# Moving one of six weight buffers 64 bytes along the partition

## The chip, the cores and the metric

The kernel runs on one core of one Trainium2 chip. The metric is the device time of one execution in microseconds (us); lower is better.

## The reference

Two layers of a first block (convolution, block attention, gated linear attention, a feed-forward part with a short convolution) run over 256 tokens of width 1024, then two layers of a second block (adaptive modulation, two feed-forward half steps, neighbourhood and windowed attention with a context of 256 tokens). Nearly all of the arithmetic is in products of the tokens with large float32 weight matrices; cut to these:

```python
def reference(x, ..., w_in, w_out, ffn_w_up, ffn_w_down, ...):
    for l in range(2):             # first block
        p = rms_norm(x, norm_mix_g[l]) @ w_in[l]
        y = mixers(p)              # convolution, block attention, linear attention
        x = x + y @ w_out[l]
        u = causal_depthwise_conv(rms_norm(x, norm_ffn_g[l]) @ ffn_w_up[l], ...)
        x = x + (silu(u[..., :2816]) * u[..., 2816:]) @ ffn_w_down[l]
    x = rms_norm(x, final_g)
    for l in range(2):             # second block, x and ctx
        x, ctx = half_step(x, ..., w_up_2[l, 0], w_down_2[l, 0]), half_step(ctx, ...)
        px, pc = modulate(norm(x)) @ w_in_2[l], modulate(norm(ctx)) @ w_in_2[l]
        attended = attention(px, pc)
        x = x + gate * (attended @ w_out_2[l])
        x = half_step(x, ..., w_up_2[l, 1], w_down_2[l, 1])
    return x
```

## The kernel before

All weight matrices are laid out by the host as one stream of 510 units of 128 partitions x 1024 float32 (512 KB each). Every unit goes through the same four steps.

- SyncE loads it into slot `g % 6` of the ring `W_raw` (`load`, L825), once TensorE is done with unit `g - 6`.
- ScalarE copies it, rounded to fp32r, into slot `g % 4` of the ring `W_hi` (`split`, L1505), once TensorE is done with unit `g - 4`.
- VectorE writes raw minus high into `W_lo` (`split`, L1881). `W_lo` has the same addresses as `W_raw`: the subtraction is in place, slot by slot.
- TensorE multiplies. The inputs are split into a high and a low part in the same way (`H_hi`, `H_lo` and `HID` of a stream, A for the tokens and B for the context), and each product of 128 x 128 weights with 256 columns of input takes three matmuls in one accumulation group (`three`, L977 to L979): low weights with high inputs, high weights with low inputs, high with high. The weights are the stationary operand, loaded by a LDWEIGHTS each, the inputs the moving one.

A visit is the use of one unit by one stream: 8 such groups of three, 24 matmuls. There are 744 visits, since many units of the second block serve both streams, A and B, in turn. In 28 visits (`token`, L1031 to L1034) the roles are swapped: the inputs are stationary and the weights move. I call these token visits and the others feature visits. Of the 744 visits 124 use a unit in the last slot (`g % 6 == 5`). TensorE runs the visits in the fixed order of the list `ORDER`, and between them it does attention and normalisation matmuls.

The addresses within a partition are written out by hand, from an aligned base. Every slot of the weight rings begins at a multiple of 4096 bytes; the input buffers begin 192 bytes past a multiple of 1024, and so does each of their rows of 256 elements:

```python
        W_hi = at("W_hi", 0, [P, HIGH, UNIT], F32R)
        W_raw = at("W_raw", 16 * K, [P, RAW, UNIT])
        W_lo = at("W_lo", 16 * K, [P, RAW, UNIT], F32R)
        AA, AB = 72 * K + 192, 124 * K + 192
        for s, h_at, x_at, arena in ((A, 40 * K + 192, 150 * K + 256, AA), (B, 56 * K + 192, 158 * K + 256, AB)):
            s.H_hi = at("H_hi" + n, h_at, [P, KT, SEQ], F32R)
            s.H_lo = at("H_lo" + n, h_at + 8 * K, [P, KT, SEQ], F32R)
            s.HID = at("HID" + n, arena, [P, 6, 2, 512], F32R)
```

The pieces of weights that a matmul loads begin at multiples of 512 bytes within the slot. So while a LDWEIGHTS reads its piece, the matmul before it reads inputs whose address is 192 bytes further on, counted modulo 512; only where a feature visit follows a token visit, or the other way round, does one pair have another distance (both operands at a multiple of 512, or both 192 past one).

Of the kernel before, what the change touches and what calls it, by code (L numbers as in the profile page):

```python
# [6 lines left out]
F32 = mybir.dt.float32  # L7
F32R = mybir.dt.float32r
# [3 lines left out]
ACT = mybir.ActivationFunctionType  # L12
AX = mybir.AxisListType

P = 128
# [12 lines left out]
UNIT = 1024  # L28
RAW = 6
HIGH = 4  # L30
# [147 lines left out]
MIX1_OUT = [1, G, 3, G, 5, G, 7, G, G, 0, 2, 4, 6]  # L178
GLUE = 13
LATE_BIAS = 6  # L180
FIRST_KV = 17
B_FIRST = {24: 21, 25: 23}
A_FIRST = {24: 3, 25: 5}
# [130 lines left out]
def make_order():  # L314
# [20 lines left out]
    def b_may():  # L335
# [5 lines left out]
        if ia < len(a) and a[ia].stage.kind == "att2" and a[ia].i == 0 and b[ib].stage.kind == "in2" \  # L341
                and b[ib].i >= FIRST_KV and (len(b[ib].stage.steps) - b[ib].i) % 3 == 0:
            return False
# [11 lines left out]
    def a_may():  # L355
# [4 lines left out]
            and not (a[ia].stage.kind == "att2" and a[ia].i == 0 and ib < len(b) and b[ib].stage.kind == "in2"  # L360
                     and not (b[ib].i >= FIRST_KV and (len(b[ib].stage.steps) - b[ib].i) % 3 == 0))

# [240 lines left out]
def build_kernel(nc, xT, ctxT, wstream, adastream, par, const, imask, cond, outT):  # L603
    with ExitStack() as ctx:  # L604
        K = 1024
# [5 lines left out]
        def at(name, off, shape, dt=F32, limit=SPACE):  # L611
            size = int(np.prod(shape[1:])) * (2 if dt == BF16 else 4)
            assert off + size <= limit - (base - whole), (name, off, size)
            return nc.alloc_sbuf_tensor_at(name, shape, dt, offset=base + off)

        W_hi = at("W_hi", 0, [P, HIGH, UNIT], F32R)
        W_raw = at("W_raw", 16 * K, [P, RAW, UNIT])
        W_lo = at("W_lo", 16 * K, [P, RAW, UNIT], F32R)
        A_raw = at("A_raw", 166 * K + 256, [P, ADA_RING, UNIT])
        PROD = at("PROD", 174 * K + 256, [P, 2, UNIT], BF16)  # L620
        SC = at("SC", 178 * K + 256, [P, 2, D])
# [16 lines left out]
        S = Semaphores(lambda name: ctx.enter_context(nc.semaphore(name)))  # L638
# [109 lines left out]
        def wait(eng, sem, value):  # L748

            if isinstance(value, int) and value <= 0:  # L750
                return
            eng.wait_ge(sem, value)
# [58 lines left out]
        @block.sync  # L811
        def _(sp):
            half = KT // 2
            sp.dma_start(A.X[:, 0:half, :], xT[:, 0:half, :]).then_inc(S.x_in, 16)
            sp.dma_start(A.X[:, half:KT, :], xT[:, half:KT, :]).then_inc(S.x_in, 16)
            sp.dma_start(CON[:, 0:CON_HEAD], const[:, 0:CON_HEAD]).then_inc(S.head_in, 16)
            sp.dma_start(PAR[:, 0:PAR_HEAD], par[:, 0:PAR_HEAD]).then_inc(S.head_in, 16)

            def load(g):

                if g >= RAW:
                    s, n = FREED[g - RAW]
                    sp.wait_ge(streams[s].sem.done, n)
                u = UNITS[g]
                sp.dma_start(W_raw[:, g % RAW, :], wstream[u * P:u * P + P, :]).then_inc(S.raw_in[g % RAW], 16)  # L825

            def load_ada(t):

                wait(sp, S.mod_sums, t - ADA_RING + 1)
                sp.dma_start(A_raw[:, t % ADA_RING, :], adastream[P * t:P * t + P, :])\  # L830
                    .then_inc(S.ada_in[t % ADA_RING], 16)

            for g in range(AHEAD):
                load(g)
            sp.dma_start(CON[:, CON_HEAD:], const[:, CON_HEAD:]).then_inc(S.con_in, 16)
            sp.dma_start(PAR[:, PAR_HEAD:], par[:, PAR_HEAD:]).then_inc(S.par_in, 16)
            for g in range(AHEAD, RAW):
                load(g)
            sp.dma_start(MASKI[:, :], imask).then_inc(S.mask_in, 16)
            sp.dma_start(SC[:, :, :], cond).then_inc(S.cond_in, 16)  # L840
            sp.dma_start(B.X[:, :, :], ctxT).then_inc(S.ctx_in, 16)
            for t in range(ADA_RING):
                load_ada(t)
            t, due = ADA_RING, 0
            for v in ORDER:
                if v.final and v.g + RAW < TOTAL["u"]:
                    load(v.g + RAW)
                if v.final:
                    for _ in range(due):
                        if t < ADA_UNITS:  # L850
                            load_ada(t)
                            t += 1
                    due = v.ada
            st = STAGES["A"][-1]
            sp.wait_ge(A.sem.evac, st.old.tok)
            sp.dma_start(outT[:, 0:half, :], A.X[:, 0:half, :]).then_inc(S.stored, 16)
            sp.wait_ge(A.sem.upd, st.upd + 1)
            sp.dma_start(outT[:, half:half + 2, :], A.X[:, half:half + 2, :]).then_inc(S.stored, 16)
            sp.wait_ge(A.sem.evac, st.old.tok + 1)
            sp.dma_start(outT[:, half + 2:KT, :], A.X[:, half + 2:KT, :]).then_inc(S.stored, 16)  # L860
            sp.wait_ge(S.stored, 48)
# [3 lines left out]
        def _(pool):  # L865
# [5 lines left out]
            def bias_table(l):  # L871

                pool.memset(BT[:, :, :], BIG).then_inc(S.bt_low, 1)
                pool.wait_ge(S.bt_low, l + 1)
                o = _par[f"rpb{l}"]
                rows = par[0:64, o:o + 48].rearrange("(h r) e -> h r e", h=2)
                for c in range(64):
                    c0 = min(max(c - 8, 0), 48)
                    r = 15 + c0 - c
                    for h in range(2):  # L880
                        pool.dma_start(BT[64 * h + c:64 * h + c + 1, c0:c0 + 16, :], rows[h:h + 1, r:r + 16, :])\
                            .then_inc(S.bt_in, 16)
# [27 lines left out]
            def ffn(s, st):  # L910
                for i in range(len(st.steps)):
                    if i == LATE_BIAS and st.blk == 1 and st.l == DEPTH - 1:
                        pool.wait_ge(s.sem.done, st.v)
                        bias_table(0)
                    if i == LATE_BIAS and s is A and st.blk == 2 and st.l == 0 and st.ffn == 1:
                        pool.wait_ge(s.sem.done, st.v)
# [35 lines left out]
        def _(pe):  # L952
# [17 lines left out]
            def weights():  # L970
                g = now.visit.g
                pe.wait_ge(S.w_lo, g + 1)
                return W_lo[:, g % RAW, :], W_hi[:, g % HIGH, :]

            def three(out, wl, wh, xl, xh, start, stop):

# [4 lines left out]
            def plain(s, st, b, q, hw):  # L981

                wl, wh = weights()
                for t in range(2):
                    for k in range(4):
                        kt = 4 * (q % 2) + k
                        if t == 0 and q < 2:
                            pe.wait_ge(s.sem.h_ready, hw(kt))
                        c = slice(256 * k + P * t, 256 * k + P * t + P)
                        mm = three(b[:, 2 * (q // 2) + t, :], wl[:, c], wh[:, c], s.H_lo[:, kt, :], s.H_hi[:, kt, :],  # L990
                                   kt == 0 and t == 0, kt == 7)
                mm.then_inc(s.sem.done, 1)

            def early(s, st, b, q):

                wl, wh = weights()
                for t in range(2):
                    for k in range(4):
                        kt = 4 * (q % 2) + k
                        if t == 0 and q < 2:  # L1000
                            pe.wait_ge(S.h0_ready, KT * st.early + kt + 1)
                        c = slice(256 * k + P * t, 256 * k + P * t + P)
                        mm = three(b[:, 2 * (q // 2) + t, :], wl[:, c], wh[:, c], H0_lo[:, kt, :], H0_hi[:, kt, :],
                                   kt == 0 and t == 0, kt == 7)
                mm.then_inc(s.sem.done, 1)
# [490 lines left out]
        def _(act):  # L1496
            def split(g):

                if g >= TOTAL["u"]:
                    return  # L1500
                act.wait_ge(S.raw_in[g % RAW], 16 * (g // RAW + 1))
                if g >= HIGH:
                    s, n = FREED[g - HIGH]
                    act.wait_ge(streams[s].sem.done, n)
                act.activation(W_hi[:, g % HIGH, :], W_raw[:, g % RAW, :], ACT.Copy).then_inc(S.w_hi, 1)  # L1505

            def evacuated(s, tok):

# [357 lines left out]
        def _(dve):  # L1866
# [9 lines left out]
            def split(g):  # L1876

                if g >= TOTAL["u"]:
                    return
                dve.wait_ge(S.w_hi, g + 1)  # L1880
                dve.tensor_tensor(W_lo[:, g % RAW, :], W_raw[:, g % RAW, :], W_hi[:, g % HIGH, :].bitcast(F32),  # L1881
                                  ALU.subtract).then_inc(S.w_lo, 1)

            def ada():
# [683 lines left out]
            for n, v in enumerate(ORDER):  # L2568
                if 2 <= n < 2 + AHEAD:
                    split(n - 2)  # L2570
                if n == FIRST_STEPS:
                    dve.wait_ge(S.par_in, 16)
                    dve.wait_ge(S.con_in, 16)
                    for l in range(DEPTH):
                        o = _par[f"sink{l}"]
# [159 lines left out]
```

## Time and profile before

| | |
|---|---|
| median of 3 runs | 2533.37 us (2530.72 to 2538.22) |
| the profiled execution | 2531.44 us |
| its span, first to last instruction | 2529.6 us |
| TensorE matmul busy | 2391.1 us, 95% |
| TensorE weight load busy | 2318.8 us, 92% |
| VectorE busy | 1660.9 us, 66% |
| ScalarE busy | 995.8 us, 39% |
| GpSimd busy | 187.9 us, 7% |
| mean granted TensorE clock | 0.967 of full speed |
| DMA | 352.78 MB, 139 GB/s on average |

The span is that of the profiled execution; what lies around it is 1.8 us. In the timeline a matmul's listed duration overlaps the next ones, so what a matmul costs is the distance from its start to the next start. The windows view counts the matmuls that run in a stretch of time, which gives the mean distance.

### The profile page before, as it was taken

Reading aid. Unit: us, or ns where it says so; the run is one execution under the profiler, and the core shown is the slowest. Engines: PE = TensorE matmul, PEld = TensorE weight load, DVE = VectorE, ACT = ScalarE, POOL = GpSimd, SP = SyncE. Lnnn points to the kernel's source line nnn. Section 1 sums busy time; section 2 is a strip of 40 time slices with the busy share of each in tenths; the row PEclk is TensorE's granted clock in tenths of the full one; section 3 lists DMA queues with packets and bytes.
Section 4 is the critical chain, followed back from the end, with each engine's and each line's share of the span. In section 5 each row is a group of like instructions: output and inputs, shape, how many; then the busy total and the mean of one; then the engine's idle time right before and its main releaser. Section 6 shows DMA issues by size and latency. Waiting matters only on the chain. (4 is left out here: it accounts for less than half of the span.)

```text
span 2529.6 us, 47682 instructions
## 1 busy us (share of the span) xinstructions
PE 2391.1 (95%) x20452; PEld 2318.8 (92%) x20452; DVE 1660.9 (66%) x2777; ACT 995.8 (39%) x1468; POOL 187.9 (7%) x300
## 2 busy tenths in 40 slices
PE   7989999899899999999789999999999999988999
PEld 7889998899899999999559999999999999966999
DVE  7778887689877767754684777775333335376554
ACT  6455554565532222232473322223322224145543
POOL 0000000190000000011001900000000000100000
PEclk9899998899989999999899999999999999989999
DMA  6246653357535555422002555552323223112454
GB/s 254 89 153 209 223 187 120 120 186 250 181 111 198 185 191 190 177 67 84 18 1 68 181 189 195 184 187 89 101 92 101 97 96 109 61 50 67 167 192 159
DMA packets 104306, 352.78 MB, mean 139 GB/s; under 512 B 18976, under 2 KB 19232, under 8 KB 103840
## 3 DMA queue, kind: packets, MB, share of 16 engines
q1 hardware_dynamic: 95904, 348.94, 40.1%
q8 instruction: 161, 2.64, 0.4%
q0 software_dynamic: 8192, 0.80, 0.3%
q14 instruction: 49, 0.40, 0.1%
HBM read 348.63 MB, written 1.05 MB: 138 GB/s over the span
## 5 line engine op out<-in xcount | busy, mean ns | idle before, releaser
L1505 ACT ACTIVATE W_hi<-W_raw 128x1024 fp32r<-128x1024 f32 x510 | 538.4, 1059 | 1078.9 <-PE slot L979 1006.1
L1881 DVE TENSOR_TENSOR W_lo<-W_raw,W_hi 128x1024 fp32r<-128x1024 f32 x510 | 622.3, 1223 | 452.5 <-ACT W_hi L1505 443.6
L977 PE MATMUL slot<-H_hiA,W_lo 128*128 128x256 f32 x2768 | 792.5, 286 | 25.4 <-DVE H_loA L2018 11.8
L978 PE MATMUL slot<-H_loA,W_hi 128*128 128x256 f32 x2768 | 781.3, 282 | 0.0
L979 PE MATMUL slot<-H_hiA,W_hi 128*128 128x256 f32 x2768 | 780.4, 282 | 0.0
L977 PEld LDWEIGHTS slot<-H_hiA,W_lo 128*128 128x128 f32 x2768 | 535.9, 194 | 39.1 <-issue 20.7
L978 PEld LDWEIGHTS slot<-H_loA,W_hi 128*128 128x128 f32 x2768 | 534.2, 193 | 0.1
L979 PEld LDWEIGHTS slot<-H_hiA,W_hi 128*128 128x128 f32 x2768 | 533.4, 193 | 0.0
L1893 DVE SCALAR_TENSOR_TENSOR PROD<-A_raw,SC 128x1024 bf16<-128x1024 f32 x288 | 341.4, 1223 | 161.1 <-DMA A_raw<-adastream 160.6
L977 PE MATMUL slot<-H_hiB,W_lo 128*128 128x256 f32 x1376 | 385.4, 280 | 3.8 <-DVE VB L2405 1.3
L979 PE MATMUL slot<-H_hiB,W_hi 128*128 128x256 f32 x1376 | 382.9, 278 | 0.0
L978 PE MATMUL slot<-H_loB,W_hi 128*128 128x256 f32 x1376 | 382.9, 278 | 0.0
L977 PE MATMUL slot<-HIDA,W_lo 128*128 128x256 f32 x1056 | 293.7, 278 | 2.2 <-DVE HIDA L2113 1.2
L978 PE MATMUL slot<-HIDA,W_hi 128*128 128x256 f32 x1056 | 293.3, 278 | 0.0
L979 PE MATMUL slot<-HIDA,W_hi 128*128 128x256 f32 x1056 | 293.3, 278 | 0.0
L977 PEld LDWEIGHTS slot<-H_hiB,W_lo 128*128 128x128 f32 x1376 | 260.6, 189 | 6.0 <-issue 2.2
L978 PEld LDWEIGHTS slot<-H_loB,W_hi 128*128 128x128 f32 x1376 | 259.5, 189 | 0.0
L979 PEld LDWEIGHTS slot<-H_hiB,W_hi 128*128 128x128 f32 x1376 | 259.0, 188 | 0.0
L977 PEld LDWEIGHTS slot<-HIDA,W_lo 128*128 128x128 f32 x1056 | 199.8, 189 | 3.0 <-DVE W_lo L1881 2.4
L979 PEld LDWEIGHTS slot<-HIDA,W_hi 128*128 128x128 f32 x1056 | 198.2, 188 | 0.0
L978 PEld LDWEIGHTS slot<-HIDA,W_hi 128*128 128x128 f32 x1056 | 198.2, 188 | 0.0
L869 POOL TENSOR_TENSOR R0A<-V_A,EXPO 128x2 f32<-128x2 f32 (+3 forms) x25 | 38.7, 1548 | 2002.6 <-DVE V_A L1919 2002.6
(277 smaller groups left out, 3059.0 us busy)
## 6 DMA issues: line engine op xcount, KB each, us to landing
W_raw<-wstream SPq DMA_DIRECT2D x510, 512.0 KB, 3.3
A_raw<-adastream SPq DMA_DIRECT2D x144, 512.0 KB, 4.5
BT<-par POOLq DMA_DIRECT2D x256, 3.0 KB, 2.7
XA<-xT SPq DMA_DIRECT2D x2, 512.0 KB, 4.6
SC<-cond SPq DMA_DIRECT2D x1, 1024.0 KB, 14.4
XB<-ctxT SPq DMA_DIRECT2D x1, 1024.0 KB, 16.3
CON<-const SPq DMA_DIRECT2D x1, 960.5 KB, 9.6
PAR<-par SPq DMA_DIRECT2D x1, 680.0 KB, 10.8
```

Source lines behind the costliest of these rows:

```text
L869: pool.tensor_tensor(s.R0[:, 0:n], s.V_[:, 0:n], EXPO[:, 0:n], ALU.pow).then_inc(s.sem.r0, 1)
L977: pe.matmul(out, wl, xh, start=start, stop=False, skip_group_check=True)
L978: pe.matmul(out, wh, xl, start=False, stop=False, skip_group_check=True)
L979: return pe.matmul(out, wh, xh, start=False, stop=stop, skip_group_check=True)
L1505: act.activation(W_hi[:, g % HIGH, :], W_raw[:, g % RAW, :], ACT.Copy).then_inc(S.w_hi, 1)
L1881: dve.tensor_tensor(W_lo[:, g % RAW, :], W_raw[:, g % RAW, :], W_hi[:, g % HIGH, :].bitcast(F32), ALU.subtract).then_inc(S.w_lo, 1)
L1893: a = dve.scalar_tensor_tensor(PROD[:, b, :], A_raw[:, slot, :], 1.0, SC[:, b, :], ALU.mult, ALU.mult, accum_out=MOD[:, t // MODS, t % MOD ...
```

## The change

The six slots of `W_raw` and `W_lo` become six tensors each. The first five stay where they were; the last, slot 5, begins 64 bytes further on. It ends 64 bytes past the multiple of 4096 at which it ended before; the next buffer, `H_hiA`, begins 192 bytes past it. The instructions, their order on every engine and their waits are the same as before; all addresses but those of slot 5 are the same.

```diff
+ASIDE = 64
...
-        W_raw = at("W_raw", 16 * K, [P, RAW, UNIT])
-        W_lo = at("W_lo", 16 * K, [P, RAW, UNIT], F32R)
+        raw_at = [16 * K + 4 * K * i + (ASIDE if i == RAW - 1 else 0) for i in range(RAW)]
+        W_raw = [at(f"W_raw{i}", o, [P, UNIT]) for i, o in enumerate(raw_at)]
+        W_lo = [at(f"W_lo{i}", o, [P, UNIT], F32R) for i, o in enumerate(raw_at)]
...
-                sp.dma_start(W_raw[:, g % RAW, :], wstream[u * P:u * P + P, :]).then_inc(S.raw_in[g % RAW], 16)
+                sp.dma_start(W_raw[g % RAW][:, :], wstream[u * P:u * P + P, :]).then_inc(S.raw_in[g % RAW], 16)
...
-                return W_lo[:, g % RAW, :], W_hi[:, g % HIGH, :]
+                return W_lo[g % RAW][:, :], W_hi[:, g % HIGH, :]
...
-                act.activation(W_hi[:, g % HIGH, :], W_raw[:, g % RAW, :], ACT.Copy).then_inc(S.w_hi, 1)
+                act.activation(W_hi[:, g % HIGH, :], W_raw[g % RAW][:, :], ACT.Copy).then_inc(S.w_hi, 1)
...
-                dve.tensor_tensor(W_lo[:, g % RAW, :], W_raw[:, g % RAW, :], W_hi[:, g % HIGH, :].bitcast(F32),
+                dve.tensor_tensor(W_lo[g % RAW][:, :], W_raw[g % RAW][:, :], W_hi[:, g % HIGH, :].bitcast(F32),
                                   ALU.subtract).then_inc(S.w_lo, 1)
```

## Rows read from the trace of the kernel before

**Rows 1.** Page, part 1: busy us, share of the span, instructions

```profile
PE 2391.1 (95%) x20452; PEld 2318.8 (92%) x20452; DVE 1660.9 (66%) x2777; ACT 995.8 (39%) x1468; POOL 187.9 (7%) x300
```

**Rows 2.** Page, part 5: the two splits of the weights, and their waits

```profile
L1505 ACT ACTIVATE W_hi<-W_raw 128x1024 fp32r<-128x1024 f32 x510 | 538.4, 1059 | 1078.9 <-PE slot L979 1006.1
L1881 DVE TENSOR_TENSOR W_lo<-W_raw,W_hi 128x1024 fp32r<-128x1024 f32 x510 | 622.3, 1223 | 452.5 <-ACT W_hi L1505 443.6
```

**Rows 3.** Windows, PE: stretch, length, busy us (matmuls), granted clock, DMA share, GB/s

```profile
186.00:346.00 160.00, 159.59 (x1355) 1.00 0.65 217
...
874.00:1066.00 192.00, 192.00 (x1632) 1.00 0.52 185
1096.00:1167.00 71.00, 71.00 (x668) 1.00 0.23 75
1402.00:1576.00 174.00, 174.00 (x1538) 1.00 0.57 196
1584.00:1740.00 156.00, 156.00 (x1327) 1.00 0.48 169
1774.00:2118.00 344.00, 343.82 (x3034) 1.00 0.29 97
```

**Rows 4.** Windows, all engines (PE, PEld, DVE, ACT, POOL), three of the same stretches

```profile
874.00:1066.00 192.00, 192.00 (x1632) 192.00 (x1631) 138.72 (x213) 47.49 (x55) 0.00 (x0) 1.00 0.52 185
1402.00:1576.00 174.00, 174.00 (x1538) 174.00 (x1537) 131.09 (x197) 46.08 (x55) 47.46 (x100) 1.00 0.57 196
1584.00:1740.00 156.00, 156.00 (x1327) 156.00 (x1326) 103.84 (x156) 40.27 (x48) 0.00 (x0) 1.00 0.48 169
```

**Rows 5.** Timeline, PE: a stretch begins after a wait (start us, us)

```profile
872.15 0.38 PE L977 MATMUL slot<-HIDA,W_lo 128*128 128x256 f32 x1 [0.70 <-DVE W_lo L1881]
```

**Rows 6.** Timeline, PE: the same stretch ends behind 12 short matmuls

```profile
1069.65 0.28 PE L979 MATMUL slot<-HIDB,W_hi 128*128 128x256 f32 x1
...
1070.01 0.28 PE L979 MATMUL slot<-HIDB,W_hi 128*128 128x256 f32 x1
1070.36 1.47 PE L1063 MATMUL slot<-CON,SQA 128*128 128x1 f32 x12
...
1072.13 0.28 PE L977 MATMUL slot<-HIDB,W_lo 128*128 128x256 f32 x1
...
1072.47 0.28 PE L977 MATMUL slot<-HIDB,W_lo 128*128 128x256 f32 x1
```

**Rows 7.** Timeline, PE: from a token visit to a feature visit, no pause

```profile
1167.07 0.28 PE L1034 MATMUL slot<-W_hi,H_hiB 128*128 128x256 f32 x1
...
1167.42 0.28 PE L1034 MATMUL slot<-W_hi,H_hiB 128*128 128x256 f32 x1
1167.54 0.28 PE L977 MATMUL slot<-H_hiA,W_lo 128*128 128x256 f32 x1
...
1167.89 0.28 PE L977 MATMUL slot<-H_hiA,W_lo 128*128 128x256 f32 x1
1168.01 0.28 PE L978 MATMUL slot<-H_loA,W_hi 128*128 128x256 f32 x1
...
1168.35 0.28 PE L978 MATMUL slot<-H_loA,W_hi 128*128 128x256 f32 x1
```

**Rows 8.** Timeline, PE: another such junction, 5 us later

```profile
1172.54 0.28 PE L1034 MATMUL slot<-W_hi,H_hiB 128*128 128x256 f32 x1
...
1172.88 0.28 PE L1034 MATMUL slot<-W_hi,H_hiB 128*128 128x256 f32 x1
1172.99 0.28 PE L977 MATMUL slot<-H_hiA,W_lo 128*128 128x256 f32 x1
...
1173.35 0.28 PE L977 MATMUL slot<-H_hiA,W_lo 128*128 128x256 f32 x1
```

**Rows 9.** Windows of the whole span, L977 (upper) and L1033 (lower): PE, PEld, clock, DMA

```profile
0.00:2529.60 2529.60, 1618.94 (x5728) 1096.22 (x5728) 0.97 0.41 139
...
0.00:2529.60 2529.60, 63.87 (x224) 43.75 (x224) 0.97 0.41 139
```

**Rows 10.** Waits of ACT: for whom, total us, times, longest

```profile
ACT W_hi L1505 <- DMA W_raw<-wstream: 19.2, 13, 2.9
```

## The prediction

> **What bounds the kernel now.** I read the page's totals first, then the windows of long stretches, then single matmuls in the timeline. TensorE is busy 95% of the span and its weight loads 92% [rows 1]; the two engines that prepare the weights spend much of their time waiting, ScalarE for TensorE (1006.1 us before its split) and VectorE for ScalarE (443.6 us) [rows 2]. So the end is set by how fast TensorE gets through its matmuls, and a few ns per matmul count.
>
> What the page doesn't show is that this pace has two values. Look at the stretches without a pause, all at a granted clock of 1.00 (the 2.4 GHz level) [rows 3]. From 1774 to 2118 us 3,034 matmuls take 343.82 us, from 1402 to 1576 us 1,538 take 174.00: 113.3 and 113.1 ns each; the starts in the timeline give 113.3 (three in 0.34 us). From 874 to 1066 us 1,632 take 192.00 and from 1584 to 1740 us 1,327 take 156.00: 117.6 ns each by the count, 117.8 by the starts, which don't count the matmuls that run over an edge. The stretch from 186 to 346 us is of the slow kind too (159.59 us for 1,355). The instructions are the same in both kinds: units, tiles and shapes don't decide it. Neither does the load on the other engines: VectorE is busy 75% of the fast stretch at 1402 (131.09 of 174) and 67% of the slow one at 1584 (103.84 of 156), and the DMA share is higher in the fast one [rows 4]. The pace is kept for some 60 to 70 visits on end and changes where TensorE paused: the slow stretch begins at 872.15 behind a wait of 0.70 us for weights [rows 5], and it ends behind twelve short normalisation matmuls, with three starts 0.36 us apart before and 0.34 after [rows 6]. I take it that weight loads and the moving reads of the matmul before fall into one of two repeating patterns, and that a pattern, once taken, holds until something disturbs it.
>
> Does an address disturb it? The trace holds a trial of it, where feature and token visits meet without a pause and one pair of reads has another distance. At 1167.54 the slow pattern (three starts in 0.35) goes over into the fast one (three in 0.34) within a few matmuls [rows 7]. At 1172.99 the fast one goes over into the slow one (0.34, then 0.36) [rows 8]. Followed through the timeline, there are 16 such junctions: of 9 entered slow 5 came out fast, of 7 entered fast 1 came out slow. No unbroken run of feature visits that I followed changed its pace by itself.
>
> **The change, part by part.** Nothing is added, removed or reordered; what changes is the address that 85 loads write, 85 copies and 85 subtractions read or write, and 992 weight loads of TensorE read (one sixth of 5,728 + 224 [rows 9], which is also 124 visits by 8).
>
> The DMA: a landing that is later by a little would be seen first as a wait of ScalarE for `W_raw`, which is 19.2 us in 13 cases now [rows 10]. The load is issued six units ahead, so I cost it at nothing. If all 85 copies waited one tenth of their own 1059 ns longer, that would be 9 us of ScalarE's time beside 1006.1 us of its waiting for TensorE [rows 2]; the same goes for the subtractions of 1223 ns. TensorE covers both, and this edit goes together with the DMA at nothing.
>
> The weight loads of TensorE themselves: no row shows a distance of 128 bytes. From below, a junction after which the fast pattern holds shows at most 2 ns more in the starts, once; from above, the loads could cost what the slow pattern costs, 117.8 - 113.3 = 4.45 ns each. That is 0 to 992 x 4.45 ns = 4.4 us. A gain below 113.3 ns isn't excluded by a reason, but the nearest case is the same size the other way, so the bounds are -4.4 and +4.4 us. I take +1 us, since 6 of 7 junctions left the fast pattern alone and that is the nearest row.
>
> The pattern is the large term. The slow one holds in three long stretches, where the windows count 1,355 + 1,632 + 1,327 = 4,314 matmuls [rows 3]; at 4.45 ns that is 19.2 us. Now the ring passes slot 5 once in six units, so each stretch meets the new distance early: the first begins two units before a slot-5 unit, the second two units before, the third in one. There are eight shifted loads in each such visit. If the slow pattern is broken with the junctions' frequency, 5 in 9, at each pass, a stretch needs 0.8 further passes on average, of six units or 12 visits: 0.8 x 12 x 24 x 4.45 ns = 1.0 us for each of three stretches, and 1 us for the way to the first passes. So 4 us of the 19.2 are kept and 15 go. The shorter slow stretches, the longest from 1096 to 1167 us with 668 matmuls and so 3.0 us [rows 3], lie between pauses and junctions that throw the dice anyway; I leave them as they are, but they and fragments of like size make up to 6 us more for the low end.
>
> Sum against the profiled execution: 2531.4 - 15 + 1 = 2517.4 us. The median of the runs shown is 1.9 us above that execution, so I forecast 2518. The spread of those runs, 7.5 us, is just what one stretch of 70 visits costs in the other pattern (70 x 24 x 4.45 ns = 7.5 us); I read from it that the pattern is thrown anew in each execution.
>
> **The rivals.** *No effect.* What the pattern depends on may be time alone, and the junctions may disturb it by their change of operand kind and not by the address. Then nothing changes: 2533 us, 2529 to 2540. In its favour: only junctions show an address effect, and there the roles change too. Against: the input buffers and weights are read by the same two paths at a junction, and one pair has another distance.
>
> The Trainium skill speaks for this rival. Its page "SBUF — State Buffer", section "Who interferes with whom", gives TensorE two independent read ports, one for the moving operand and one for the weight load, and says "PE and ACT never wait on anyone." By that rule no address would matter and the sum would be the time before. This case's trace doesn't quite agree, since it holds two paces of identical instructions at one clock, 113.3 and 117.8 ns; but it doesn't show that addresses are the cause.
>
> *Slot 5 throws the fast pattern into the slow one.* This is the case of the junction at 1172.99. Most of the time is fast now: with 17,856 matmuls on weights, of which some 5,600 start in the slow pattern, about a third is slow. If passes through slot 5 throw either way with equal odds, half would be slow: 0.18 x 17,000 x 4.45 ns = 14 us more, 2545 us. It decides against the change from the point where a pass breaks the fast pattern half as often as the slow one (1/3 slow is the balance of odds 1 to 2); by the junctions it is 1 in 7 against 5 in 9, a ratio of one quarter, from few cases. At worst every pass leaves the slow pattern behind: 11,400 fast matmuls by 4.45 ns, 51 us, 2584 us.
>
> *The distance of 128 bytes has a pace of its own.* At up to 4.45 ns for 992 loads it adds 4.4 us, and alone that would be 2537 us; it widens each case and isn't one of its own.
>
> **How the numbers follow.** The slow pattern is broken and the fast one holds: 0.45, around 2518. No effect: 0.25. Slot 5 makes slow of fast: 0.30. The low end takes all of the slow pattern gone, 19.2 + 6 = 25 us, so 2507. The high end takes the equal odds of the second rival with the loads' own 4.4 us, 2550; the tail to 2584 is left out with about one in ten. The likeliest case's own range is 2507 to 2526. A measurement of this kernel can tell about 0.3% (7.6 us) from no change. Faster by more than that: 0.46; within: 0.26; slower: 0.28.
>
> **What would show it.** In the windows of the changed kernel 113.3 ns per matmul should hold in the long joint stretches (roughly 870 to 1070 and 1580 to 1740 us), with the slow pattern ending in or just behind a visit to slot 5. The weight loads of slot 5 should show the same distances as the others within 2 ns. It is wrong if long stretches at 117.8 ns run on across slot-5 visits (no effect), or if a stretch turns slow in such a visit (second rival), or if the first start distances in slot-5 visits differ by more than 4.45 ns (third). VectorE's, ScalarE's and the DMA's rows should be those of before.

## The result and the profile after

The changed kernel took 2547.26 us (median of 5 executions, 2542.27 to 2552.28), the kernel before 2533.37 us (2523.37 to 2544.49, 5 executions in all). The ratio is 1.0075 with a 95% interval of 1.0044 to 1.0106: slower by three quarters of a per cent, where I had forecast 0.6% faster. The profiled execution took 2552.28 us, with a span of 2550.5 us; that is 20.9 us more than the span before. In the 55 further executions of the kernel before that were timed beside the experiments the median is 2529.65 us, and three of them are above the changed kernel's median, so the loss doesn't hang on the five of the first comparison.

Page of the changed kernel, parts 1 and 5 (line numbers are two higher than before, so L979, L980 and L981 are the L977, L978 and L979 of the rows above):

```profile
PE 2412.9 (95%) x20452; PEld 2342.6 (92%) x20452; DVE 1660.4 (65%) x2777; ACT 996.0 (39%) x1468; POOL 187.9 (7%) x300
...
L1507 ACT ACTIVATE W_hi<-W_raw 128x1024 fp32r<-128x1024 f32 x510 | 538.2, 1059 | 1103.2 <-PE slot L981 1035.7
L1883 DVE TENSOR_TENSOR W_lo<-W_raw,W_hi 128x1024 fp32r<-128x1024 f32 x510 | 621.6, 1222 | 466.3 <-ACT W_hi L1507 457.5
```

TensorE is busy 21.8 us longer with the same number of instructions [rows 1]. The two splits take the same time as before, to 1 ns, and wait longer for TensorE [rows 2]. ScalarE's wait for loads is shorter than before [rows 10]:

```profile
ACT W_hi L1507 <- DMA W_raw<-wstream: 14.1, 10, 3.3
```

So the loss is on TensorE alone, and the windows show its kind. In the kernel before, the stretch from 1774 to 2118 us held the fast pace, 113.3 ns, throughout [rows 3]. Windows of the changed kernel (stretch, length, busy us and matmuls, granted clock, DMA share, GB/s), first from the stretch around 750 us, then later:

```profile
736.00:752.00 16.00, 16.00 (x144) 1.00 0.59 196
752.40:769.20 16.80, 16.80 (x145) 1.00 0.53 188
769.40:785.60 16.20, 16.20 (x145) 1.00 0.56 196
```

```profile
188.00:346.00 158.00, 157.26 (x1352) 1.00 0.66 222
1402.00:1576.00 174.00, 173.43 (x1489) 1.00 0.55 190
1790.00:2118.00 328.00, 328.00 (x2822) 1.00 0.29 95
```

No pace holds for long. From 736 to 752 us TensorE starts a matmul every 113.3 ns, from 752.4 to 769.2 every 118 ns, then fast again, in a rhythm of 33 us, which is one turn of the six-slot ring for both streams. (These paces are those of the starts in the timeline. The count of a window this short takes in two or three matmuls that run over its edges, so dividing gives 111.1 and 115.9 ns.) In the long window from 1790 to 2118 us the mean is 116.2 ns, between the two paces, since both alternate there. The turning points are visits to slot 5. The timeline of the changed kernel at the end of one such visit, and at the start of the next (start us, us):

```profile
735.17 0.28 PE L981 MATMUL slot<-H_hiB,W_hi 128*128 128x256 f32 x1
...
735.52 0.28 PE L981 MATMUL slot<-H_hiB,W_hi 128*128 128x256 f32 x1
...
735.88 0.28 PE L981 MATMUL slot<-H_hiB,W_hi 128*128 128x256 f32 x1
736.00 0.28 PE L979 MATMUL slot<-H_hiA,W_lo 128*128 128x256 f32 x1
...
736.34 0.28 PE L979 MATMUL slot<-H_hiA,W_lo 128*128 128x256 f32 x1
...
736.68 0.28 PE L979 MATMUL slot<-H_hiA,W_lo 128*128 128x256 f32 x1
...
751.98 0.28 PE L979 MATMUL slot<-H_hiB,W_lo 128*128 128x256 f32 x1
...
752.32 0.28 PE L979 MATMUL slot<-H_hiA,W_lo 128*128 128x256 f32 x1
...
752.68 0.28 PE L979 MATMUL slot<-H_hiA,W_lo 128*128 128x256 f32 x1
...
753.03 0.28 PE L979 MATMUL slot<-H_hiA,W_lo 128*128 128x256 f32 x1
```

The visit that ends at 736.00 uses slot 5: its groups of three are 0.35 to 0.36 us apart, and from the next visit's first matmul on it is 0.34. At 752.32 stream A begins the next unit of slot 5, and at once the distance is 0.36 and 0.35 again. Followed through the whole timeline, this is no throw of dice. A pass is one visit to slot 5, with the visits before and behind it. Of 101 passes with no pause on either side, 52 were entered in the slow pattern and every one was left in the fast one; 49 were entered fast and every one was left slow. The slot-5 visit itself ran at about 118.2 ns in all of them; that is a mean of start distances that go from 114 to 124 ns and repeat, where the fast pattern has 113 or 114 throughout. Of the 744 visits 434 were slow in this execution, against 234 in the profiled one of before: 200 x 24 matmuls x 4.45 ns = 21.4 us, which is the 20.9 us of the span within the error of this count.

### The profile page after: what moved, and what is told of

Read it like the earlier page. It is cut to its first block and busy times, and to the rows that moved or that the text cites. A ratio compares the mean times of both kernels' runs of the same rounds, so it can differ in the third digit from the quotient of the medians.

```text
span 2550.5 us, 47682 instructions
## 1 busy us (share of the span) xinstructions
PE 2412.9 (95%) x20452; PEld 2342.6 (92%) x20452; DVE 1660.4 (65%) x2777; ACT 996.0 (39%) x1468; POOL 187.9 (7%) x300
## 5 line engine op out<-in xcount | busy, mean ns | idle before, releaser
L979 PE MATMUL slot<-H_hiA,W_lo 128*128 128x256 f32 x2768 | 797.2, 288 | 25.3 <-DVE H_loA L2020 11.3
L980 PE MATMUL slot<-H_loA,W_hi 128*128 128x256 f32 x2768 | 787.0, 284 | 0.0
L981 PE MATMUL slot<-H_hiA,W_hi 128*128 128x256 f32 x2768 | 785.9, 284 | 0.0
L979 PEld LDWEIGHTS slot<-H_hiA,W_lo 128*128 128x128 f32 x2768 | 535.4, 193 | 39.1 <-issue 21.6
L981 PEld LDWEIGHTS slot<-H_hiA,W_hi 128*128 128x128 f32 x2768 | 539.1, 195 | 0.0
L980 PEld LDWEIGHTS slot<-H_loA,W_hi 128*128 128x128 f32 x2768 | 535.7, 194 | 0.1
L979 PE MATMUL slot<-H_hiB,W_lo 128*128 128x256 f32 x1376 | 387.0, 281 | 3.4 <-DVE VB L2407 1.3
L980 PE MATMUL slot<-H_loB,W_hi 128*128 128x256 f32 x1376 | 385.5, 280 | 0.0
L981 PE MATMUL slot<-H_hiB,W_hi 128*128 128x256 f32 x1376 | 385.2, 280 | 0.0
L979 PE MATMUL slot<-HIDA,W_lo 128*128 128x256 f32 x1056 | 294.6, 279 | 1.5 <-DVE HIDA L2115 1.1
L980 PE MATMUL slot<-HIDA,W_hi 128*128 128x256 f32 x1056 | 294.9, 279 | 0.0
L981 PE MATMUL slot<-HIDA,W_hi 128*128 128x256 f32 x1056 | 294.7, 279 | 0.0
L979 PEld LDWEIGHTS slot<-H_hiB,W_lo 128*128 128x128 f32 x1376 | 259.9, 189 | 5.6 <-issue 2.1
L981 PEld LDWEIGHTS slot<-H_hiB,W_hi 128*128 128x128 f32 x1376 | 261.8, 190 | 0.0
L980 PEld LDWEIGHTS slot<-H_loB,W_hi 128*128 128x128 f32 x1376 | 259.8, 189 | 0.0
L979 PEld LDWEIGHTS slot<-HIDA,W_lo 128*128 128x128 f32 x1056 | 198.7, 188 | 2.0 <-DVE W_lo L1883 2.0
L981 PEld LDWEIGHTS slot<-HIDA,W_hi 128*128 128x128 f32 x1056 | 200.1, 190 | 0.0
L980 PEld LDWEIGHTS slot<-HIDA,W_hi 128*128 128x128 f32 x1056 | 198.2, 188 | 0.0
```

Of the source, the lines that this page charges most:

```text
L979: pe.matmul(out, wl, xh, start=start, stop=False, skip_group_check=True)
L980: pe.matmul(out, wh, xl, start=False, stop=False, skip_group_check=True)
L981: return pe.matmul(out, wh, xh, start=False, stop=stop, skip_group_check=True)
```

## The experiments

Every kernel below is the changed one with the edit shown, or that with the move set to 0. "Distance" is the input's address minus the weight piece's, modulo 256 bytes: 192 everywhere in the kernel before, 128 for the low weights of slot 5 in the changed one. The executions of the kernel before beside them ran from 2508.08 to 2555.15 us, with medians of 2526.8 to 2530.4 us in the four batches. Each kernel has one profile; counts of visits and passes are of that execution, and of a few visits in each the pace can't be told, because pauses break them up. The ratios stand as recorded with their intervals; where a kernel ran four times, dividing its median by the batch's gives up to 0.4% more (0.992 in place of 0.988 for the move of slot 5 by 128 bytes).

The spread of the kernel before fits a pattern that is settled anew in each execution. That is inferred, since one execution of it was profiled; but three of the kernels below behave like it, and the four profiles have about 235, 150, 300 and 415 slow visits in spans of 2529.6, 2519.4, 2531.4 and 2543.7 us. Taking off each span what its visits took above 113.3 ns a matmul leaves 2500 to 2505 us. The same done with all fourteen profiles of this document leaves 2491 to 2505 us of spans that go from 2502 to 2585, so the paces of the visits account for most of the differences. The profile of each kernel says more than its time.

**Undo the part that TensorE sees.** The raw slot stays moved, the low weights go back to the old place, for VectorE that writes them and for TensorE that reads them:

```diff
-        W_lo = [at(f"W_lo{i}", o, [P, UNIT], F32R) for i, o in enumerate(raw_at)]
+        W_lo = [at(f"W_lo{i}", 16 * K + 4 * K * i, [P, UNIT], F32R) for i in range(RAW)]
```

> Slot 5 of the raw weights stays 64 bytes further on, but the low weights of slot 5 are written back to the old address, so the loads, copies and subtractions have the new address and TensorE the old one. Theory A (TensorE's weight loads of slot 5 at a distance of 128 instead of 192 bytes from the inputs switch the pattern): long stretches at one pace return, as before, no change of pace in slot-5 visits, time about 2533 us, between 2523 and 2545. Theory B (the writes by DMA, or ScalarE's and VectorE's reads at the new address, disturb TensorE): the pace goes on alternating at every slot-5 unit, some 430 of 744 visits slow, time about 2547 us.

2534.64 us (2521.24 to 2555.10), ratio 1.0019 (0.9982 to 1.0055). The alternation is gone: of 101 passes with known patterns on both sides 81 were fast before, in and behind slot 5, 19 slow in all three, and one changed. Windows of this kernel:

```profile
540.00:680.00 140.00, 139.59 (x1189) 1.00 0.68 223
```

```profile
1790.00:2118.00 328.00, 327.21 (x2881) 1.00 0.29 99
```

The first lies, all but its last 11 us, in a slow stretch that begins at 521 us and runs across a slot-5 visit every 17 us or so (117.4 ns by the count); the second, with 113.6 ns, is fast throughout. Patterns hold again, one as well as the other. The loads write, ScalarE's copies read and VectorE's subtractions read the moved address in this kernel just as in the changed one, so theory B falls for these three. VectorE's writes went back together with TensorE's reads, and this edit doesn't part them; the timeline of the changed kernel does. The subtraction that fills slot 5 for the visits of 752.32 (stream A) and 766.47 (stream B) is this one:

```profile
748.95 1.22 DVE L1883 TENSOR_TENSOR W_lo<-W_raw,W_hi 128x1024 fp32r<-128x1024 f32 x1
```

It is over at 750.17, and TensorE stays fast for 2 us more, up to the first matmul of stream A's visit. Stream B's visit turns the pattern back, and the next write to slot 5 begins only at 783.97. One write, two turns, each at a visit: so it is TensorE's reading of the moved weights that alternates.

**Move everything together.** All slots back in line, the base of all buffers 64 bytes further on:

```diff
-ASIDE = 64
+ASIDE = 0
...
-        base = (whole + 127) // 128 * 128
+        base = (whole + 127) // 128 * 128 + 64
```

> No slot is moved against the others; every buffer of the kernel begins 64 bytes further on. Theory A (the distance between weights and inputs counts): nothing changes, long stretches at 113.3 or 117.8 ns, about 2533 us. Theory B (the absolute address modulo 128 or 256 bytes counts, for instance of the row that a weight load starts in): the pace is another one throughout, by up to 17000 matmuls x 4.45 ns = 76 us either way, or the patterns break up.

2530.60 us (2512.37 to 2549.66), ratio 0.9986 (0.9942 to 1.0030). Both paces occur and hold: 117.6 ns over 186 us in one stretch, 113.3 ns over 328 us in another.

```profile
874.00:1060.00 186.00, 186.00 (x1581) 1.00 0.53 187
1790.00:2118.00 328.00, 328.00 (x2896) 1.00 0.29 97
```

Moving everything by 64 bytes doesn't matter; moving the weights alone by as much does. It is the distance that counts.

**The same distance in all slots.** Low weights and raw weights of all six slots 64 bytes further on:

```diff
-        raw_at = [16 * K + 4 * K * i + (ASIDE if i == RAW - 1 else 0) for i in range(RAW)]
+        raw_at = [16 * K + 4 * K * i + ASIDE for i in range(RAW)]
```

> All six slots of raw and low weights are moved by 64 bytes, so each group of three matmuls has one low load at the distance 128 and two high loads at 192, in every visit. Theory A (this distance has a pattern of its own near the slow pace): all visits run like the slot-5 visits of the changed kernel, about 118.1 ns per matmul, no visit at 113.3, time about 2531 + 51 = 2582 us or a little more. Theory B (only the change of distance from one visit to the next switches the pattern): once uniform, a pattern holds again for long stretches, both paces occur, about 2533 us.

2581.28 us (2577.88 to 2587.06), ratio 1.0180 (1.0124 to 1.0236). Theory A's 2582 us. None of the visits is at 113.3 ns, nearly all are at 118.2 or 118.3. Windows of this kernel:

```profile
188.00:346.00 158.00, 157.64 (x1333) 1.00 0.64 219
1790.00:2118.00 328.00, 327.83 (x2773) 1.00 0.28 92
```

327.83 / 2,773 is 118.2 ns. With this distance in every slot there is no alternation; feature visits with low loads at distance 128 beside high loads at 192 showed no fast pattern at all.

**Another distance in slot 5.** The move is 128 bytes:

```diff
-ASIDE = 64
+ASIDE = 128
```

> Only slot 5 moved, by 128 bytes instead of 64: distance 64 to the inputs. Theory A1 (any odd slot switches the pattern at each pass): alternation at each slot-5 unit as with 64 bytes, about 2547 us. Theory A2 (what a pass does depends on the distance): another outcome, either all fast after a few passes, about 2508 us, or all slow, about 2584 us.

2506.38 us (2504.74 to 2509.98), ratio 0.9884 (0.9831 to 0.9938): faster than both kernels. The slow pattern is broken and the fast one left alone, as I had forecast for 64 bytes, and the time is at the low end of my 2507 to 2526 us. The timeline of this kernel where a slow stretch meets slot 5:

```profile
189.22 0.28 PE L979 MATMUL slot<-H_hiA,W_lo 128*128 128x256 f32 x1
...
189.58 0.28 PE L979 MATMUL slot<-H_hiA,W_lo 128*128 128x256 f32 x1
...
189.93 0.28 PE L979 MATMUL slot<-H_hiA,W_lo 128*128 128x256 f32 x1
...
190.28 0.28 PE L979 MATMUL slot<-H_hiA,W_lo 128*128 128x256 f32 x1
...
190.62 0.28 PE L979 MATMUL slot<-H_hiA,W_lo 128*128 128x256 f32 x1
...
190.96 0.28 PE L979 MATMUL slot<-H_hiA,W_lo 128*128 128x256 f32 x1
```

At 189.93 a slot-5 visit begins; its first group of three still takes 0.35 us, from the second on it is 0.34 and stays so. In the kernel before, this stretch was slow for 160 us [rows 3]. Of 99 passes without a pause 89 were fast before, in and behind slot 5, and 7 turned from slow to fast at its beginning. The three that were slow in slot 5 are token visits. 67 visits were slow in all. This span is 25.8 us shorter than that of before; the visits account for 167 x 24 x 4.45 ns = 17.8 us of it. The granted clock of this execution was 0.974, of the one before 0.967, so part of the rest is less time at the 1.2 GHz level; in the other three executions, at 0.969 to 0.971, the kernel took 2504.74 to 2509.98 us all the same.

**Between 0 and 64.** The same with 32 bytes:

```diff
-ASIDE = 64
+ASIDE = 32
```

> Only slot 5 moved, by 32 bytes: distance 160. If the effect goes in steps of 64 bytes of address, either nothing changes against before (long stretches, 2510 to 2550 us) or it is as with 64 bytes (alternation, 2547 us). If it is continuous, something between: slot-5 visits with paces other than 113.3 and 117.8 to 118.1 ns.

2540.50 us (2527.84 to 2547.85), ratio 1.0026 (0.9993 to 1.0060). A third kind: from the fast pattern 67 passes ran their slot-5 visit at 118.7 ns and came out fast; from the slow one 29 stayed slow, slot-5 visit and all, at 117.8. Windows of this kernel, a slow stretch and a fast one:

```profile
188.00:346.00 158.00, 157.25 (x1337) 1.00 0.65 219
1790.00:2118.00 328.00, 328.00 (x2873) 1.00 0.29 97
```

The second gives 114.2 ns: five visits in six at 113.3 and one at 118.7. Neither the kernel before nor that with 64 bytes does this, so addresses count in steps of less than 64 bytes.

**All low slots at the good distance, and all weights at one distance.** Low and raw by 128, then low, raw and high by 64, and all three by 128. The first edit is that of the kernel with 64 bytes in all slots, with `ASIDE = 128`; the other two have, besides,

```diff
-        W_hi = at("W_hi", 0, [P, HIGH, UNIT], F32R)
+        W_hi = at("W_hi", ASIDE, [P, HIGH, UNIT], F32R)
```

> All six slots of raw and low weights 128 bytes further on: the low loads are at distance 64 in every visit, the high loads at 192. Theory A (a load at distance 64 breaks the slow pattern and leaves the fast one alone): no slow stretch survives anywhere, also not the short ones between pauses that one slot left, below 2506 us, about 2500 us (67 slow visits less, 67 x 24 x 4.45 ns = 7 us). Theory B (it takes the change of distance on entering and leaving the slot): long stretches hold again, both paces occur, 2510 to 2550 us.

> High, raw and low weights all 64 bytes further on: every weight load at distance 128. Theory A (the fast pattern needs most loads away from distance 128): no visit at 113.3 ns, 118 ns or more, 2582 us or above. Theory B (what hurts is that low and high loads have different distances): one distance for all gives two holding patterns again, 2510 to 2550 us.

> High, raw and low weights all 128 bytes further on: every weight load at distance 64. Theory A (distance 64 favours the fast pattern): all visits fast, about 2500 us. Theory B (only the mixture of 64 and 192 breaks the slow pattern): both patterns hold for long stretches, 2510 to 2550 us.

Low by 128: 2506.88 us (2506.40 to 2509.83), ratio 0.9894 (0.9813 to 0.9974), with 34 slow visits. Theory A's 2500 us wasn't reached. With one slot moved 67 visits had been slow, so half of them went, but the time stayed the same. Of the 34 that are left 27 are token visits: all 27 whose pace can be told are slow here, against 15 of 27 in the kernel before. Of the feature visits hardly any is slow, so for these theory A holds, and it failed for the visits with swapped roles. All weights by 64: 2587.73 us (2586.24 to 2594.91), ratio 1.0223 (1.0138 to 1.0308), at 118.7 ns. All by 128: 2567.27 us (2564.90 to 2568.19), ratio 1.0131 (1.0063 to 1.0199); 42 visits fast, the rest at 117.8. Here it is the other way round: 21 of 27 token visits are fast, and 21 of some 700 feature visits. In a token visit the moving weights lie 192 bytes before the stationary inputs, not behind them, so what a placement does to feature visits needn't hold for them; the table below is for feature visits. One window each, of low by 128 (in the repeat below), all by 64 and all by 128, each from its own kernel:

```profile
1402.00:1576.00 174.00, 173.80 (x1534) 1.00 0.55 195
```

```profile
1790.00:2118.00 328.00, 327.42 (x2745) 0.99 0.27 91
```

```profile
1790.00:2118.00 328.00, 328.00 (x2788) 1.00 0.28 94
```

That is 113.3, 119.3 (with 3.4 us at the lower clock; 118.7 by the starts without them) and 117.6 ns. Theory B of the last two, one distance for all gives both patterns back for long, falls; so does theory A of the last, that a distance of 64 favours the fast pattern by itself. Of the placements run it did so only for low loads at 64 beside high loads at 192. The two kernels also rule out that the place of low and high weights against each other is all that counts: it is the same in both as in the kernel before, and the paces are not.

**Distance 0.** Low and raw by 192 in all slots, and in slot 5 alone (`ASIDE = 192` in the two forms shown):

> All six slots of raw and low weights 192 bytes further on: the low loads are at distance 0, the high loads at 192. At distance 128 (64 bytes further) all visits were slow, at 64 (128 bytes further) nearly all fast. Theory A (what helps is a low load two or more 64-byte steps from the high loads' distance): fast again, about 2507 us. Theory B (each distance is a case of its own): no forecast; 2506 to 2585 us, and the pace of the long stretches tells which of the kinds it is.

> Only slot 5 moved, by 192 bytes: distance 0. If a pass does in one slot what the same distance does in all six (as 64 bytes: all slow in six slots, passes that leave the slow pattern behind or undo it in one; 128 bytes: fast in both), the outcome follows the run with all six slots at this distance; else distance and alternation are separate matters.

All slots: 2585.12 us (2582.01 to 2587.12), ratio 1.0215 (1.0162 to 1.0268). No visit is fast; feature visits have again two patterns, one at 117.8 and one at 122.2 ns, the slowest seen. Windows of this kernel, one in each:

```profile
188.00:346.00 158.00, 157.59 (x1338) 1.00 0.65 220
1790.00:2118.00 328.00, 327.83 (x2683) 1.00 0.27 91
```

Slot 5 alone: 2565.48 us (2562.08 to 2568.91), ratio 1.0141 (1.0095 to 1.0186). Of 101 passes 90 stayed slow, 10 went from fast to slow, and one came out fast. 647 visits were slow. This is the extreme of my second rival: one odd slot is enough to hold nearly the whole kernel in the slow pattern. Theory A of the first run, that two or more steps of 64 bytes help, falls.

**How far does the distance reach?** Weights as before, all else 256 bytes further on:

```diff
-            return nc.alloc_sbuf_tensor_at(name, shape, dt, offset=base + off)
+            return nc.alloc_sbuf_tensor_at(name, shape, dt, offset=base + off + (0 if name[:2] == "W_" else 256))
```

> All weight slots where they were in the kernel before, every other buffer 256 bytes further on: the distance from the weights to the inputs is 448 bytes modulo 512, but still 192 modulo 256. Theory A (distances count modulo 256 bytes): as before, both patterns hold for long stretches in feature visits, 113.3 and 117.8 ns, 2508 to 2555 us. Theory B (modulo 512 or more): another kind, seen by paces other than these two, or by only one of them throughout; 2505 or 2565 us and above.

2534.26 us (2519.97 to 2545.51), ratio 1.0007 (0.9978 to 1.0037). Both patterns, both long, with the paces of before. Windows of this kernel:

```profile
1402.00:1576.00 174.00, 174.00 (x1538) 1.00 0.56 194
1790.00:2118.00 328.00, 328.00 (x2788) 1.00 0.28 94
```

The first gives 113.1 ns and the second 117.6. Moving the inputs by 256 bytes changed nothing that these runs can tell, so the distance counts modulo 256, while 32 and 64 bytes make a difference.

**The best version again.** Low and raw by 128 in all slots, in more executions:

> The best version so far (all low and raw slots 128 bytes further on) against the kernel before in more executions: 2500 to 2512 us in each, against 2508 to 2555 for the kernel before; ratio about 0.99, the interval clear of 1.

2505.51 us (2500.95 to 2509.33, 6 executions) against 2530.24 us (2519.04 to 2547.02, 11), ratio 0.9902 (0.9866 to 0.9938). One per cent faster than the kernel before, and with a third of its spread (8.4 us against 28.0). Between this and slot 5 alone by 128 the runs show no difference.

What the placements come to in feature visits, with the high loads at 192 unless said otherwise:

| low distance | in all slots | in slot 5 alone |
|---|---|---|
| 192 (before) | 113.3 or 117.8 ns, both hold | the same |
| 160 | not run | 118.7 in the slot, pattern kept, 2540.5 us |
| 128 | 118.2, 2581.3 us | 118.2 in the slot, pattern swapped, 2547.3 us |
| 64 | 113.3, 2505.5 us | slow turned into fast, 2506.4 us |
| 0 | 117.8 or 122.2, 2585.1 us | fast turned into slow, 2565.5 us |
| 128, high too | 118.7, 2587.7 us | not run |
| 64, high too | mostly 117.8, 2567.3 us | not run |

## Why the prediction was wrong

- *TensorE's pace sets the end, and it has two values.* Right. The page after shows no other engine slower, and the spans differ by what the visits' paces add up to.
- *The address of the weights relative to the inputs disturbs the pattern.* Right, and now shown: moving both together changes nothing, moving TensorE's view back takes the effect away. The "no effect" rival falls with that: kernels with the same instructions in the same order ran from 2505.5 to 2587.7 us by the place of their weights alone. The page of the Trainium skill that spoke for this rival ("SBUF — State Buffer", "Who interferes with whom") calls TensorE's two read ports independent and says that it never waits on anyone. Against other engines no run here contradicts it. As I used it, for TensorE's own two reads, it doesn't agree with these times.
- *Costs of DMA, copies and subtractions: nothing.* Right [rows 2, 10]; the kernel that moves only their address took 2534.64 us.
- *The shifted loads themselves: +1 us, at most 4.4.* Mis-sized. I priced the eight shifted loads of a visit alone. But a visit with them runs as a whole at a mean of 118.2 ns, all 24 matmuls, with single start distances up to 124 ns: 4.9 ns x 24 x 124 visits would be 14.6 us if all of them had been fast before. My sign that slot 5 would show the others' distances within 2 ns failed too.
- *"If the slow pattern is broken with the junctions' frequency, 5 in 9", and the fast one left alone in 6 of 7.* This is the step that failed. Slot 5 is no single disturbance like a junction. It is eight equal ones, and what comes out is fixed: slow goes in and fast comes out, 52 of 52; fast goes in and slow comes out, 49 of 49. I took frequencies from cases with another distance (0) and a change of roles, and let them decide for a distance of which no row existed. Had I priced the swap, it would have read: half of the 620 visits outside slot 5 slow and all 124 in it, 434 of 744. That it is the number measured to the last digit is chance, since pauses reset the pattern too; that it is close is not.
- *"A stretch needs 0.8 further passes on average, of six units or 12 visits."* One visit in six uses slot 5, in the joint stretches too, where each stream passes it once a turn; so passes are six visits apart on average and this term should have been half as large. It is 1.5 us in all and doesn't change the outcome.
- *The second rival* came nearest, with its price of 14 us and 2545 us; measured 2547.3. It had slot 5 make slow of fast, but as a throw with equal odds: half of the visits slow, where the swap gives half outside slot 5 and all within. The range up to 2550 us holds the measured time for this rival's sake alone; the mechanism that I put forward gave 2507 to 2526 us. It had a chance of 0.30 and should have had at least that of the forecast, since no row had the new distance. The runs show how open it was: of the four moves tried in slot 5 one is faster, two are slower and one is about the same.
- *The saving of 15 us from breaking long slow stretches* was right in size for a kernel that I hadn't predicted: with 128 bytes instead of 64 the visits account for 17.8 us.

What stays open is why. The runs show which distances have a fast pattern; they don't show what makes it, in the memory or in TensorE, and I have only the start distances to go by. Nor do they show why the pattern behind a slot-5 visit is fixed by the one before it. Distance 96, those between 0 and 64, and moves of the high loads alone weren't run.

## What to carry to other kernels

When a TensorE-bound kernel repeats identical matmuls, look at the time from start to start, not at busy shares: the share was 94 to 95% in kernels from 2505 to 2588 us. Two values a few per cent apart at the same granted clock are the sign. The relative place of stationary and moving operands in a partition then is a parameter to be measured, kind by kind, at a step below 64 bytes over a range of 256; here it couldn't be interpolated, since low distances of 64 and 0, neighbours in steps of 64, gave 2505.5 and 2585.1 us. Token visits answered otherwise than feature visits, so each role is to be looked at by itself. A layout with a single pattern also takes most of the spread out of the executions (8 us in six executions of the best version, 26 to 43 in the 11 to 19 of the kernel before in each batch), which makes later changes easier to measure.

## What was not expected of the hardware

TensorE's mean time from start to start for 128 x 128 weights and 256 columns took the values 113.3, 117.8, 118.2, 118.7 and 122.2 ns at a granted clock of 1.00, by addresses alone. The first is even (113 or 114 ns each time), the last three are means of unequal start distances that repeat (117, 122 and 127 or 128 ns in turn for 122.2). With one placement, two of them (113.3 and 117.8, or 117.8 and 122.2) each held for 150 to 370 us of the same instructions, and which one it was was settled behind a pause, or where token and feature visits meet [rows 5 to 8]. And a visit with eight shifted loads turned one pattern into the other both ways, 101 times of 101 in the profiled execution.
